# Joining the four chunks of an SSD scan into one stage schedule, and moving a state decay from VectorE to ScalarE

## The chip, the cores and the metric

The kernel runs on all 8 cores of one Trainium2 chip. Each core works on its own prompt sequence (2048 tokens) and its own 16 sample tokens, with the same weights. The metric is the device time of the slowest core in microseconds (us).

## What is computed

One layer of a hybrid decoder. Three mixers (a short gated convolution A, a Mamba-2 SSD branch B, a cross-attention C) read the same normalised input, are gated and merged, and a SwiGLU block follows. The change touches branch B alone. For the prompt it is a scan over chunks of 128 tokens:

```python
lmat = jnp.exp(jnp.where(causal, seg, -jnp.inf))
cb = jnp.einsum('bcign,bcjgn->bcijg', cr, br)
y_diag = jnp.einsum('bcijg,bcijgh,bcjghp->bcighp', cb, lmat, xdt)
def carry_step(s, inp):
    st, dec = inp
    return s * dec[..., None, None] + st, s
y_off = jnp.einsum('bcign,bcghpn,bcigh->bcighp', cr, s_prev, jnp.exp(acum))
```

For each sample token it is one step of the same recurrence, on a state of 32 heads x 64 x 128:

```python
s = s * jnp.exp(dtt * a)[..., None, None] + (dtt[..., None] * xt)[..., None] * bh[:, :, None, :]
return s, jnp.einsum('bhpn,bhn->bhp', s, ch)
```

## The kernel before

**Order.** The prompt is worked in four tiles of 512 tokens (`tile`): branch A, branch C, branch B, merge, SwiGLU, each fed by weight slabs that `wload` (L338) loads into a ring of 16 pages from POOL's queue. After the four tiles `sample` works on the 16 sample tokens. Instructions are added one by one through helpers (L344 `mm`, L347 `tr`, L355 `act`, L358 `tt`, L362 `ts`), so most rows of the trace bear a helper's line and are told apart by their tiles. Each engine runs its own instructions strictly in the order in which they were added. `Sched.add` sets a semaphore wait for each conflict of keys. For two instructions on one engine other than PE the wait is left out when they lie more than 6 places apart; two neighbours that write the same key do wait for each other. Whoever reads a PSUM bank also takes a lock on it (`psx`), so two readers of one bank follow each other.

**The scan in a tile** (in `branchB`). NS = 4 chunks `j`, and in each 4 groups `g4` of 8 heads. At the head of a chunk PE forms the four B.C products in bank 7 and ScalarE copies them to `CBs`. Then 14 steps `u` follow, and in each the stages are added in the order S5, S4, S3, S2, S1, A. In words:

- A(t), t = 0 to 7 (two per group): PE multiplies C by the carried state `Sbf` into bank `bo` (for even t), then one masked and three further products into bank 4 or 5; ScalarE takes the exponential into `Lt`; VectorE multiplies it by `CBs` into `MT`. The third buffer of `Lt` and `MT` is a piece of the tile `xdd`, so one in three shows under that name.
- S1(t), two steps later: PE multiplies `MT` by the inputs into bank `by`.
- S2(g): VectorE scales `bo` into `sA` (this frees `bo`), adds `by`, adds the skip term `sB` and multiplies by the gate into `yb`. POOL makes `sB`, the state input `xddg` and the decayed state `Sf`.
- S3(g): ScalarE squares `yb` into `sB` with a sum, then VectorE and ScalarE form the inverse root (`stat`). In this text "Square(k)" is the start of this squaring (`sB<-yb` on ScalarE) for the k-th group of the tile, k = 0 to 15.
- S4(g): ScalarE normalises into `ynb`; PE forms the state update in bank 7 and transposes `ynb` into bank 6.
- S5(g): VectorE adds the update to `Sf`, ScalarE copies it to `Sbf`, and VectorE and ScalarE move the four transposed blocks by turns to `G2`/`G3` (names `G<-ps,nw`).

S2 of group g is added in step 2g+4, S3 in 2g+5, S4 in 2g+6, S5 in 2g+7, so that the last steps of a chunk (u = 10 to 13) have neither S1 nor A. The next chunk's head comes behind them. After the fourth chunk come the output product with `w_ssm_out` and its gates.

**The sample state loop** (L1149 to L1171). For each of the 16 tokens: SyncE loads the next token's state (1 MB) into one of two buffers; PE broadcasts B and C into PSUM; VectorE multiplies the state by its decay into `t1_` (one instruction, `HB<-HB,G`); VectorE multiplies B by dt.x into `t2` (`MG<-ps,G`); POOL adds `t2` to `t1_` (`HB<-HB,MG`) and issues the store of the new state; VectorE multiplies by C into the same `t2` (`MG<-HB,ps`) and reduces it to `Ys` (L1171). There are two `t1_` buffers and one `t2`.

Of the kernel before, what the change touches and what calls it, by code (L numbers as in the profile page):

```python
# [8 lines left out]
AF = mybir.ActivationFunctionType  # L9
ALU = mybir.AluOpType  # L10
# [156 lines left out]
def build(with_sample=True, dbg=None, ntiles=NT, branches='ACB', stop=0):  # L167
# [95 lines left out]
    BT = sb("BT", [128, 4, T], BF16)  # L263
# [237 lines left out]
    def tile(ti, last):  # L501
# [126 lines left out]
        def branchB():  # L628
# [82 lines left out]
            BY = [0, 1]  # L711
            BO = [2, 3]
            BL = [4, 5]
            for j in range(NS):
                zk = [("zs", j, c) for c in range(4)]
                bc_ = 7
                for g4 in range(4):
                    mm(PS[bc_][:, g4 * 128:(g4 + 1) * 128], BT[:, g4, j * 128:(j + 1) * 128], CT[:, g4, j * 128:(j + 1) * 128], True, True,
                       [("BT", g4), ("CT", g4)], ("ps", bc_))
                cp("act", CBs[:].rearrange("p g i -> p (g i)"), PS[bc_][:, :], [("ps", bc_)], ["CBs"])  # L720

                def stageA(t, j=j):
                    g4, half = t // 2, t % 2
                    by, bo = BY[g4 % 2], BO[g4 % 2]
                    if half == 0:
                        mm(PS[bo][:, :], CT[:, g4, j * 128:(j + 1) * 128], Sbf[:, g4 * 512:(g4 + 1) * 512], True, True,
                           [("CT", g4), ("Sbf", g4)], ("ps", bo))
                    li = t % 3
                    bl = BL[t % 2]
                    h0 = g4 * 8 + half * 4  # L730
                    mm(PS[bl][:, :], ident_b, fap(mneg_b, [[0, 4], [1, 128]]), True, False, ["cstb"], ("ps", bl))
                    mm(PS[bl][:, :], ident_b, fap(nbh4[:, j, h0:h0 + 1], [[1, 4], [0, 128]]), False, False, ["cstb", ("nbh", j)], ("ps", bl))
                    mm(PS[bl][:, :], ident_b, fap(nbl4[:, j, h0:h0 + 1], [[1, 4], [0, 128]]), False, False, ["cstb", ("nbh", j)], ("ps", bl))
                    for hh in range(4):
                        h = h0 + hh
                        mm(PS[bl][:, hh * 128:(hh + 1) * 128], fap(dtab[:, j, h:h + 1], [[0, 128]]), tri_b, False, hh == 3,
                           [("dtab", j), "cstb"], ("ps", bl))
                    act(Lt[li][:].rearrange("p a b -> p (a b)"), PS[bl][:, :], AF.Exp, [("ps", bl)], [("Lt", li)])
                    tt("dve", MT[li][:], Lt[li][:], fap(CBs[:, g4, 0:1], [[0, 4], [1, 128]]), ALU.mult, [("Lt", li), "CBs"], [("MT", li)])

                def S1(t, j=j):
                    g4, half = t // 2, t % 2
                    by = BY[g4 % 2]
                    li = t % 3
                    for hh in range(4):
                        h = g4 * 8 + half * 4 + hh
                        hl = half * 4 + hh
                        mm(PS[by][:, hl * 64:(hl + 1) * 64], MT[li][:, hh, :], xs_v[:, j, h * 64:(h + 1) * 64], True, True,
                           [("MT", li)] + xsk, ("ps", by))

                def S2(g4, j=j, zk=zk):
                    by, bo = BY[g4 % 2], BO[g4 % 2]
                    i = g4 % 2
                    tt("dve", sA[i][:, :].rearrange("p (h q) -> p h q", h=8), PS[bo][:, :].rearrange("p (h q) -> p h q", h=8),
                       fap(eac4[:, j, g4 * 8:g4 * 8 + 1], [[1, 8], [0, 64]]), ALU.mult, [("ps", bo), ("eac4", j)], [("sA", i)])
                    tt("dve", sA[i][:, :], sA[i][:, :], PS[by][:, :], ALU.add, [("sA", i), ("ps", by)], [("sA", i)])
                    tt("pool", sB[i][:, :].rearrange("p (h q) -> p h q", h=8), xs_v[:, j, g4 * 512:(g4 + 1) * 512].rearrange("p (h q) -> p h q", h=8),
                       fap(hp[:, 2, g4 * 8:g4 * 8 + 1], [[1, 8], [0, 64]]), ALU.mult, xsk + ["hp"], [("sB", i)])
                    tt("dve", sA[i][:, :], sA[i][:, :], sB[i][:, :], ALU.add, [("sA", i), ("sB", i)], [("sA", i)])
                    tt("dve", yb[i][:, :], sA[i][:, :], zs_v[:, j, g4 * 512:(g4 + 1) * 512], ALU.mult, [("sA", i)] + zk, [("yb", i)])  # L760
                    xg = xddg[i]
                    tt("pool", xg[:].rearrange("p (h q) -> p h q", h=8), xs_v[:, j, g4 * 512:(g4 + 1) * 512].rearrange("p (h q) -> p h q", h=8),
                       fap(dsd4[:, j, g4 * 8:g4 * 8 + 1], [[1, 8], [0, 64]]), ALU.mult, xsk + [("dsd4", j)], [("xddg", i)])
                    tt("pool", Sf[:, g4 * 512:(g4 + 1) * 512].rearrange("p (h q) -> p h q", h=8),
                       Sf[:, g4 * 512:(g4 + 1) * 512].rearrange("p (h q) -> p h q", h=8),
                       fap(eac4[:, j, 32 + g4 * 8:32 + g4 * 8 + 1], [[1, 8], [0, 64]]), ALU.mult, [("Sf", g4), ("eac4", j)], [("Sf", g4)])

                def S3(g4):
                    i = g4 % 2
                    act(sB[i][:, :], yb[i][:, :], AF.Square, [("yb", i)], [("sB", i), ("gss", i)], accum=stat[:, 8 + i:9 + i])  # L770
                    rstd_from_ssq(8 + i, 12 + i, 512, 128, ("gss", i))

                def S4(g4, j=j):
                    i = g4 % 2
                    act(ynb[i][:, :], yb[i][:, :], AF.Copy, [("yb", i), ("gss", i)], [("ynb", i)], scale=stat[:, 12 + i:13 + i])
                    mm(PS[7][:, :], Btok[:, j, g4, :], xddg[i][:], True, True, ["Btok", ("xddg", i)], ("ps", 7))
                    pT = PS[6][:].bitcast(BF16)
                    for q in range(4):
                        tr(pT[:, q * 128:(q + 1) * 128], ynb[i][:, q * 128:(q + 1) * 128], ident_b, [("ynb", i), "cstb"], ("ps", 6))

                def S5(g4, j=j):
                    pT = PS[6][:].bitcast(BF16)
                    tt("dve", Sf[:, g4 * 512:(g4 + 1) * 512], Sf[:, g4 * 512:(g4 + 1) * 512], PS[7][:, :], ALU.add,
                       [("Sf", g4), ("ps", 7)], [("Sf", g4)])
                    cp("act", Sbf[:, g4 * 512:(g4 + 1) * 512], Sf[:, g4 * 512:(g4 + 1) * 512], [("Sf", g4)], [("Sbf", g4)])
                    for q in range(4):
                        ch = g4 * 4 + q
                        dstb = G2 if ch < 8 else G3
                        dk = ("G2" if ch < 8 else "G3", ch % 8)
                        if q % 2 == 0:  # L790
                            ts("dve", dstb[:, ch % 8, j * 128:(j + 1) * 128], pT[:, q * 128:(q + 1) * 128], nw[:, ch:ch + 1], None,
                               ALU.mult, None, [("ps", 6), "nw"], [dk])
                        else:
                            act(dstb[:, ch % 8, j * 128:(j + 1) * 128], pT[:, q * 128:(q + 1) * 128], AF.Copy, [("ps", 6), "nw"], [dk],
                                scale=nw[:, ch:ch + 1])

                for u in range(14):
                    for g4 in range(4):
                        if u == 2 * g4 + 7:
                            S5(g4)  # L800
                    for g4 in range(4):
                        if u == 2 * g4 + 6:
                            S4(g4)
                    for g4 in range(4):
                        if u == 2 * g4 + 5:
                            S3(g4)
                    for g4 in range(4):
                        if u == 2 * g4 + 4:
                            S2(g4)
                    if 2 <= u < 10:  # L810
                        S1(u - 2)
                    if u < 8:
                        stageA(u)
            if last:
                for q in range(16):
                    b = nb()
# [85 lines left out]
    def sample():  # L902
# [249 lines left out]
        for bi in range(P):  # L1152
            if bi + 1 < P:
# [5 lines left out]
            mm(PS[bB][:, :], oh, bctok[:, 0:512], True, True, ["cstf", "bctok"], ("ps", bB))  # L1159
            bC = nb()  # L1160
            mm(PS[bC][:, :], oh, bctok[:, 512:1024], True, True, ["cstf", "bctok"], ("ps", bC))
            tt("dve", t1_.rearrange("p (a n) -> p a n", a=16), St_.rearrange("p (a n) -> p a n", a=16),
               fap(decT[:, 0, bi:bi + 1], [[16, 16], [0, 128]]), ALU.mult, [sk_, "decsT"], [tk_])
            tt("dve", fap(t2[:, 0:1], [[512, 4], [128, 4], [1, 128]]), fap(PS[bB][:, 0:1], [[128, 4], [0, 4], [1, 128]]),
               fap(dtT[:, 0, bi:bi + 1], [[64, 4], [16, 4], [0, 128]]), ALU.mult, [("ps", bB), "dtsT"], ["t2"])
            tt("pool", t1_, t1_, t2, ALU.add, [tk_, "t2"], [tk_])
# [129 lines left out]
```

How the kernel before makes its waits and increments, by code:

```python
        def run(e, eng):  # L120
            water = {}
            for op in self.by_eng[e]:
                need = {}
                for o in op.deps:
                    k = o.sem.num
                    if water.get(k, 0) >= o.val:
                        continue
                    if k not in need or need[k][1] < o.val:
                        need[k] = (o.sem, o.val)
                for k, (s, v) in need.items():
                    eng.wait_ge(s, v)
                    water[k] = v
                ins = op.fn(eng)
                if op.is_dma:
                    ins.then_inc(op.sem, 16)
                elif op.signal:
                    ins.then_inc(op.sem, 1)
            if e == "sp":
                for s, cnt in self.slot_count.items():
                    eng.wait_ge(ssem[s], 16 * cnt)
```

## Time and profile before

| | us |
|---|---|
| median of 2 runs | 3812.38 (3811.84 to 3812.92) |
| profiled execution | 3815.4 |
| its span on the slowest core (7) | 3813.9 |
| spans of the other cores | 3745.8 to 3808.3 |
| PE busy in it | 2273.0 (60%) |
| VectorE, ScalarE, POOL busy | 1231.7, 959.6, 770.2 |

The profiled execution lies 3 us above the median, and 1.5 us of it lie outside the span. Times in the rows are microseconds from the start of the span of core 7. In a row of the timeline the columns are: start, length, engine, line, operation, output and inputs, shapes, count, and in brackets how long the engine had sat idle and who released it.

### The profile page before, as it was taken

What the parts mean: (1) busy time and instruction counts of PE and PEld (TensorE: products, weight loads), DVE (VectorE), ACT (ScalarE), POOL (GpSimd) and SP (SyncE); (2) the same over time, 40 slices, a digit from 0 to 9 for tenths busy, and PEclk for the clock granted to TensorE, in tenths of its full rate; (3) what the DMA queues carried; (4) which work ended last, traced back from release to release, by engine and by line L of the source; (5) the groups of instructions that cost most, each with busy time, mean ns of one, the idle gap of its engine ahead of it and who ended that gap; (6) DMA issues with size and microseconds to landing.
All of it is one profiled execution on the core that took longest, in us unless ns stands there. A gap on an engine that the chain in (4) does not pass through costs nothing.

```text
span 3813.9 us, 39632 instructions; the slowest of 8 cores (3745.8 to 3813.9 us)
## 1 busy us (share of the span) xinstructions
PE 2273.0 (60%) x11878; PEld 1046.6 (27%) x11878; DVE 1231.7 (32%) x2656; ACT 959.6 (25%) x2088; POOL 770.2 (20%) x759
## 2 busy tenths in 40 slices
PE   4778457758784578679646777793488322232112
PEld 2333223223332233234322333342233210120011
DVE  2224542122245321322452213335421114346610
ACT  2134431111344210223441112343311103310000
POOL 1211221312103222211132302103213010013310
PEclk8889668879886689789767888896688655555555
DMA  8974037979630489997007999750289696575498
GB/s 148 110 88 64 1 40 90 116 119 124 87 46 1 50 95 125 127 112 111 2 1 90 90 125 139 95 77 1 35 107 122 109 157 204 166 136 154 138 156 132
DMA packets 615311, 370.48 MB, mean 97 GB/s; under 512 B 394768, under 2 KB 586768, under 8 KB 615088
## 3 DMA queue, kind: packets, MB, share of 16 engines
q0 software_dynamic: 584752, 286.10, 61.1%
q1 hardware_dynamic: 30352, 81.85, 6.6%
q8 instruction: 101, 1.65, 0.2%
q14 instruction: 106, 0.87, 0.1%
HBM read 608.44 MB, written 29.14 MB: 167 GB/s over the span
## 4 chain that ended last, share of the span: by engine, by line
DMA 35%; PE 30%; DVE 12%; issue 11%; ACT 7%; POOL 3%; DVEq 1%; SPq 0%; ACTq 0%; POOLq 0%
PE ps L344 29%; DMA WRb<-w_in 13%; DMA WRb<-w_ffn_gate 6%; DMA WRb<-w_ffn_down 5%; DMA WRb<-w_ffn_up 4%; DVE MG L358 3%; DVE sA L358 2%; DMA WRb<-w_sc_out 2%; DMA WRb<-w_ssm_out 2%; POOL HB L358 2%; PE ps L347 1%; POOL WRb L338 1%; ACT sB L355 1%; DVE acs L1080 1%; DMA ostg<-st_sconv 1%
## 5 line engine op out<-in xcount | busy, mean ns | idle before, releaser
L344 PE MATMUL ps<-G,WRb 128*128 128x512 bf16 (+2 forms) x6432 | 1251.0, 350 | 363.6 <-DMA WRb<-w_in 151.8
L344 PEld LDWEIGHTS ps<-G,WRb 128*128 128x128 bf16 x6432 | 542.4, 102 | 1028.1 <-issue 531.9
L338 POOL DMA_DIRECT2D WRb<-w_in x269 | 235.9, 886 | 1458.9 <-PE ps L344 839.5
L355 ACT ACTIVATE sA<-ps 128x512 f32<-128x512 f32 (+1 forms) x294 | 142.7, 486 | 868.3 <-PE ps L344 848.7
L344 PE MATMUL ps<-WRb,HB 128*128 128x512 bf16 x960 | 232.1, 408 | 54.0 <-DMA WRb<-w_ffn_down 36.0
L355 ACT ACT_TABLE_LOAD x56 | 71.8, 1283 | 404.5 <-DVE eac L364 229.1
L358 POOL TENSOR_TENSOR sB<-HB,hp 128x512 f32<-128x512 bf16 x64 | 66.7, 1041 | 518.4 <-ACT sB L355 411.8
L358 DVE TENSOR_TENSOR HB<-sA,ps 128x512 bf16<-128x512 f32 x88 | 60.5, 688 | 342.5 <-PE ps L344 336.8
L347 PE MATMUL ps<-cstb,ynb 128*128 128x128 bf16 x256 | 34.9, 284 | 216.0 <-ACT ynb L355 159.5
L355 ACT ACTIVATE junk<-X 128x1024 bf16<-128x1024 f32 (+1 forms) x53 | 56.0, 1056 | 383.8 <-DVE X L358 306.7
L344 PEld LDWEIGHTS ps<-WRb,HB 128*128 128x128 bf16 x960 | 98.5, 104 | 187.6 <-issue 90.9
L358 DVE TENSOR_TENSOR sB<-sA,ps 128x512 f32<-128x512 f32 (+1 forms) x80 | 46.7, 584 | 302.9 <-ACT sA L355 275.6
L344 PE MATMUL ps<-WRb,G 128*128 128x512 bf16 (+3 forms) x728 | 138.0, 350 | 9.6 <-DMA WRb<-w_merge_o 8.6
L347 PE MATMUL ps<-cstb,xnb 128*128 128x128 bf16 (+1 forms) x152 | 17.9, 292 | 208.7 <-DVE xnb L373 208.7
L358 DVE TENSOR_TENSOR X<-X,ps 128x512 f32<-128x512 f32 (+1 forms) x68 | 46.7, 687 | 287.9 <-PE ps L344 287.9
L358 DVE TENSOR_TENSOR MG<-HB,ps 128x1024 f32<-128x1024 f32 (+1 forms) x48 | 75.7, 1577 | 170.2 <-POOL HB L358 78.4
L338 POOL DMA_DIRECT2D WRb<-w_ffn_up x94 | 85.6, 911 | 210.3 <-DMA WRb<-w_ffn_gate 183.8
L344 PE MATMUL ps<-X,cstf 16*128 16x512 f32 x64 | 62.3, 1103 | 107.0 <-DVE MG L358 107.0
L344 PE MATMUL ps<-xb,dg 128*128 128x512 bf16 x384 | 102.7, 391 | 26.2 <-DVE xb L370 18.5
L338 POOL DMA_DIRECT2D WRb<-w_ffn_gate x94 | 85.7, 912 | 132.2 <-PE ps L344 72.2
L362 DVE TENSOR_SCALAR dg<-cstb,cw 128x128 bf16<-128x128 bf16 x384 | 100.0, 260 | 32.4 <-DVE dg L362 2.0
L358 POOL TENSOR_TENSOR HB<-HB,MG 128x2048 f32<-128x2048 f32 x16 | 71.7, 4483 | 170.8 <-DVE MG L358 170.8
(183 smaller groups left out, 2980.4 us busy)
## 6 DMA issues: line engine op xcount, KB each, us to landing
WRb<-w_in POOLq DMA_DIRECT2D x72, 1024.0 KB, 13.0
WRb<-w_in POOLq DMA_DIRECT2D x192, 256.0 KB, 9.1
WRb<-w_ffn_down POOLq DMA_DIRECT2D x20, 1408.0 KB, 12.7
WRb<-w_ffn_gate POOLq DMA_DIRECT2D x88, 256.0 KB, 15.6
WRb<-w_ffn_up POOLq DMA_DIRECT2D x88, 256.0 KB, 15.7
WRb<-w_ssm_out POOLq DMA_DIRECT2D x20, 1024.0 KB, 11.1
HB<-cache_k SPq DMA_DIRECT2D x16, 1024.0 KB, 6.2
HB<-cache_v SPq DMA_DIRECT2D x16, 1024.0 KB, 8.6
```

The source lines that it names most:

```text
L338: S.add("pool", lambda g: g.dma_start(out=dst, in_=src), writes=[("wl", ser)] + [("wl", q) for q in prev], slot=("w", start))
L344: S.add("pe", lambda g: g.matmul(out, lhsT, rhs, start=start, stop=stop), reads=reads, writes=[pskey])
L347: S.add("pe", lambda g: g.transpose(out, in_, idn), reads=reads, writes=[pskey])
L355: S.add("act", lambda g: g.activation(out=out, in_=in_, func=func, scale=scale, **kw), reads=reads, writes=writes)
L358: S.add(eng, lambda g: g.tensor_tensor(out=out, in0=in0, in1=in1, op=op), reads=reads, writes=writes)
L362: S.add(eng, lambda g: g.tensor_scalar(out=out, in0=in0, scalar1=s1, scalar2=None, op0=op0), reads=reads, writes=writes)
L1080: S.add("dve", lambda g: g.tensor_reduce(out=ssc, in_=prod.rearrange("p (a d) -> p a d", d=256), op=ALU.add, axis=AX), reads=["prod"], wri ...
```

## The change

The first part keeps each stage of the scan, but collects them for all four chunks and runs one step counter U over the tile, U = 0 to 39: A of chunk j in steps 8j to 8j+7, S1 two steps behind it, S2 to S5 of group g of chunk j in steps 8j + 2g + 4 to 8j + 2g + 7. The chunk's head (`pro`) is added in step 8j between S1 and A; it now uses bank 4, which is also that of A(0), in place of bank 7, which S4 and S5 use. The index of the `Lt`/`MT` buffers runs on through the tile.

The second part replaces VectorE's one multiplication of the 128x2048 state by 16 ScalarE activations of 128x128, each with its own per-partition scale.

```diff
--- before.py
+++ after.py
@@ -711,13 +711,16 @@
             BY = [0, 1]
             BO = [2, 3]
             BL = [4, 5]
+            CH = []
             for j in range(NS):
                 zk = [("zs", j, c) for c in range(4)]
-                bc_ = 7
-                for g4 in range(4):
-                    mm(PS[bc_][:, g4 * 128:(g4 + 1) * 128], BT[:, g4, j * 128:(j + 1) * 128], CT[:, g4, j * 128:(j + 1) * 128], True, True,
-                       [("BT", g4), ("CT", g4)], ("ps", bc_))
-                cp("act", CBs[:].rearrange("p g i -> p (g i)"), PS[bc_][:, :], [("ps", bc_)], ["CBs"])
+
+                def pro(j=j):
+                    bc_ = BL[0]
+                    for g4 in range(4):
+                        mm(PS[bc_][:, g4 * 128:(g4 + 1) * 128], BT[:, g4, j * 128:(j + 1) * 128], CT[:, g4, j * 128:(j + 1) * 128], True, True,
+                           [("BT", g4), ("CT", g4)], ("ps", bc_))
+                    cp("act", CBs[:].rearrange("p g i -> p (g i)"), PS[bc_][:, :], [("ps", bc_)], ["CBs"])
 
                 def stageA(t, j=j):
                     g4, half = t // 2, t % 2
@@ -725,7 +728,7 @@
                     if half == 0:
                         mm(PS[bo][:, :], CT[:, g4, j * 128:(j + 1) * 128], Sbf[:, g4 * 512:(g4 + 1) * 512], True, True,
                            [("CT", g4), ("Sbf", g4)], ("ps", bo))
-                    li = t % 3
+                    li = (8 * j + t) % 3
                     bl = BL[t % 2]
                     h0 = g4 * 8 + half * 4
                     mm(PS[bl][:, :], ident_b, fap(mneg_b, [[0, 4], [1, 128]]), True, False, ["cstb"], ("ps", bl))
@@ -741,7 +744,7 @@
                 def S1(t, j=j):
                     g4, half = t // 2, t % 2
                     by = BY[g4 % 2]
-                    li = t % 3
+                    li = (8 * j + t) % 3
                     for hh in range(4):
                         h = g4 * 8 + half * 4 + hh
                         hl = half * 4 + hh
@@ -794,23 +797,20 @@
                             act(dstb[:, ch % 8, j * 128:(j + 1) * 128], pT[:, q * 128:(q + 1) * 128], AF.Copy, [("ps", 6), "nw"], [dk],
                                 scale=nw[:, ch:ch + 1])
 
-                for u in range(14):
-                    for g4 in range(4):
-                        if u == 2 * g4 + 7:
-                            S5(g4)
-                    for g4 in range(4):
-                        if u == 2 * g4 + 6:
-                            S4(g4)
-                    for g4 in range(4):
-                        if u == 2 * g4 + 5:
-                            S3(g4)
-                    for g4 in range(4):
-                        if u == 2 * g4 + 4:
-                            S2(g4)
-                    if 2 <= u < 10:
-                        S1(u - 2)
-                    if u < 8:
-                        stageA(u)
+                CH.append((pro, stageA, S1, S2, S3, S4, S5))
+            for U in range(8 * NS + 8):
+                for st_i, off in ((6, 7), (5, 6), (4, 5), (3, 4)):
+                    for j in range(NS):
+                        for g4 in range(4):
+                            if U == 8 * j + 2 * g4 + off:
+                                CH[j][st_i](g4)
+                gt = U - 2
+                if 0 <= gt < 8 * NS:
+                    CH[gt // 8][2](gt % 8)
+                if U < 8 * NS:
+                    if U % 8 == 0:
+                        CH[U // 8][0]()
+                    CH[U // 8][1](U % 8)
             if last:
                 for q in range(16):
                     b = nb()
@@ -1159,8 +1159,9 @@
             mm(PS[bB][:, :], oh, bctok[:, 0:512], True, True, ["cstf", "bctok"], ("ps", bB))
             bC = nb()
             mm(PS[bC][:, :], oh, bctok[:, 512:1024], True, True, ["cstf", "bctok"], ("ps", bC))
-            tt("dve", t1_.rearrange("p (a n) -> p a n", a=16), St_.rearrange("p (a n) -> p a n", a=16),
-               fap(decT[:, 0, bi:bi + 1], [[16, 16], [0, 128]]), ALU.mult, [sk_, "decsT"], [tk_])
+            for a16 in range(16):
+                act(t1_[:, a16 * 128:(a16 + 1) * 128], St_[:, a16 * 128:(a16 + 1) * 128], AF.Copy, [sk_, "decsT"], [tk_],
+                    scale=decT[:, a16, bi:bi + 1])
             tt("dve", fap(t2[:, 0:1], [[512, 4], [128, 4], [1, 128]]), fap(PS[bB][:, 0:1], [[128, 4], [0, 4], [1, 128]]),
                fap(dtT[:, 0, bi:bi + 1], [[64, 4], [16, 4], [0, 128]]), ALU.mult, [("ps", bB), "dtsT"], ["t2"])
             tt("pool", t1_, t1_, t2, ALU.add, [tk_, "t2"], [tk_])
```

## Rows read from the trace of the kernel before

**Rows 1.** The page: busy us, share of the span and instructions by engine.

```profile
PE 2273.0 (60%) x11878; PEld 1046.6 (27%) x11878; DVE 1231.7 (32%) x2656; ACT 959.6 (25%) x2088; POOL 770.2 (20%) x759
```

**Rows 2.** The page: the chain that ended last, by engine.

```profile
DMA 35%; PE 30%; DVE 12%; issue 11%; ACT 7%; POOL 3%; DVEq 1%; SPq 0%; ACTq 0%; POOLq 0%
```

**Rows 3.** Windows, first chunk's span: busy us (instructions) by engine, PEclk, DMA share, GB/s.

```profile
382.10:424.30 42.20, 19.27 (x124) 10.77 (x125) 21.56 (x45) 17.52 (x44) 12.98 (x12) 0.66 0.00 1
```

**Rows 4.** Timeline, ScalarE: the Squares of chunk 1, the next, and chunk 4's.

```profile
393.83 0.63 ACT L355 ACTIVATE sB<-yb 128x512 f32<-128x512 f32 x1 [0.48 <-DVE yb L358]
...
403.61 0.62 ACT L355 ACTIVATE sB<-yb 128x512 f32<-128x512 f32 x1
...
412.23 0.62 ACT L355 ACTIVATE sB<-yb 128x512 f32<-128x512 f32 x1
...
419.44 0.62 ACT L355 ACTIVATE sB<-yb 128x512 f32<-128x512 f32 x1
...
434.27 0.63 ACT L355 ACTIVATE sB<-yb 128x512 f32<-128x512 f32 x1 [0.47 <-DVE yb L358]
...
515.12 0.63 ACT L355 ACTIVATE sB<-yb 128x512 f32<-128x512 f32 x1 [0.33 <-issue]
...
524.19 0.62 ACT L355 ACTIVATE sB<-yb 128x512 f32<-128x512 f32 x1
...
532.82 0.62 ACT L355 ACTIVATE sB<-yb 128x512 f32<-128x512 f32 x1
...
539.23 0.62 ACT L355 ACTIVATE sB<-yb 128x512 f32<-128x512 f32 x1
```

**Rows 5.** Timeline, all engines: what lies between the first two Squares of chunk 1.

```profile
396.91 0.59 PE L347 MATMUL ps<-cstb,ynb 128*128 128x128 bf16 x4 [3.16 <-ACT ynb L355]
...
397.77 0.59 PE L344 MATMUL ps<-Sbf,CT 128*128 128x512 bf16 x1
...
400.16 0.60 ACT L355 ACTIVATE Lt<-ps 128x512 bf16<-128x512 f32 x1 [3.39 <-PE ps L344]
...
401.20 0.68 DVE L358 TENSOR_TENSOR Sf<-Sf,ps 128x512 f32<-128x512 f32 x1
```

**Rows 6.** Timeline, PE to ScalarE: the same stage A at the higher clock.

```profile
391.31 0.38 PE L344 MATMUL ps<-Sbf,CT 128*128 128x512 bf16 x1 [1.72 <-DVE sA L358]
...
392.76 0.60 ACT L355 ACTIVATE Lt<-ps 128x512 bf16<-128x512 f32 x1 [2.87 <-PE ps L344]
```

**Rows 7.** Timeline, a chunk's head: the B.C products, their copy, the next product.

```profile
382.14 0.58 PE L344 MATMUL ps<-CT,BT 128*128 128x128 bf16 x4 [1.52 <-DVE acs L370]
...
382.82 0.60 ACT L355 ACTIVATE CBs<-ps 128x512 bf16<-128x512 f32 x1 [0.20 <-PE ps L344]
```

**Rows 8.** Timeline, one token of the sample state loop.

```profile
3426.84 4.48 POOL L358 TENSOR_TENSOR HB<-HB,MG 128x2048 f32<-128x2048 f32 x1 [7.29 <-DVE MG L358]
...
3431.91 1.18 POOL L1167 DMA_DIRECT2D sssm<-HB  x1 [0.59 <-POOL HB L358]
...
3436.15 2.28 DVE L358 TENSOR_TENSOR HB<-HB,G 128x2048 f32<-128x2048 f32 x1
3438.35 2.28 DVE L358 TENSOR_TENSOR MG<-ps,G 128x2048 f32<-128x2048 f32 x1
```

**Rows 9.** The tile HB in that loop: ns min/median/max, first and last start.

```profile
L358 DVE TENSOR_TENSOR HB<-HB,G x16: 2279/2281/2291, 3408.2 to 3617.6; 128x2048 f32<-128x2048 f32 x16
L358 POOL TENSOR_TENSOR HB<-HB,MG x16: 4482/4483/4487, 3412.9 to 3622.5; 128x2048 f32<-128x2048 f32 x16
```

**Rows 10.** Groups of ScalarE by shape: busy us, mean ns.

```profile
L355 ACT ACTIVATE G<-ps,nw 128x128 bf16<-128x128 bf16 x128 | 46.2, 361 | 44.4 <-DVE G L362 34.0 <-PE ps L344 9.6 <-PE ps L347 0.8
```

**Rows 11.** Timeline, ScalarE: two neighbours that take turns on one bank.

```profile
3165.15 0.37 ACT L355 ACTIVATE ostg<-ps 1x256 f32<-1x256 f32 x1 [0.99 <-PE ps L344]
3165.62 0.16 ACT L355 ACTIVATE stat<-ps 1x1 f32<-1x1 f32 x1
```

**Rows 12.** The tile HB again: from issue to landing, loads and stores.

```profile
DMA to landing us min/median/max: 6.0/6.1/10.4
```

## Prediction

> **What bounds the kernel now.** First the page. No engine is near full, PE is busy 60% [rows 1], and the chain that ended last is DMA 35%, PE 30%, VectorE 12% [rows 2]: long stages wait for weights, others for products. Shares alone say nothing of the two places that the change touches, so these are read from the timeline.
>
> The first place is the scan of branch B, four times (once a tile). The window over its first chunk, 42.2 us, has PE busy 19.3, VectorE 21.6, ScalarE 17.5 and POOL 13.0 us, and no DMA [rows 3]. Nobody is the bound by work; a chain that hops between engines is. I measure it by the distance between Squares [rows 4]: 9.78, 8.62, 7.21, and then 14.83 us over the chunk's border. The 14.83 is what the change goes for: the pipe drains and fills again. The other twelve borders and inner gaps repeat this; the sixteen gaps from a chunk's first Square to its second run from 8.97 to 9.78 (first and last in tile 1: 9.78 and 9.07), eleven within 0.03 of 9.77, one 9.70, four at the end of a tile 8.97 to 9.32, mean 9.59. In a tile Square(0) to Square(15) takes 539.23 - 393.83 = 145.4; over the four tiles the mean is 145.0.
>
> The second place is the sample state loop. A token is one closed chain: POOL's add, VectorE's product with C, the reduction, the decay product, the B product, POOL's add again [rows 8]. Its period is (3622.5 - 3412.9) / 15 = 13.97 us [rows 9]. ScalarE does nothing there.
>
> **Part 1, the joined scan.** No work is removed. What decides is how long a gap between Squares is when the stages A are present all the time. The rows show one such gap in each chunk, the first one, since it holds the exponentials of A(5) and A(6); the second gap holds A(7) alone, the third none. I follow the gap of chunk 1 from its Square at 393.83 [rows 4]. The sum, root and odd exponential on ScalarE, then `MT` and `sA` on VectorE free the bank `bo`, and PE's product with the state starts at 397.77, after 3.94. The further products let the even exponential start at 400.16, after 2.39; behind it `MT`, and `Sf` starts at 401.20, after 1.04 [rows 5]. The copy to `Sbf` and the four moves to `G2`/`G3` by turns lead to the next Square at 403.61, after 2.41 [rows 4]. The sum is 9.78. In the new order every middle gap has this chain.
>
> The one variable link is PE's. From the state product to the exponential it is 400.16 - 397.77 = 2.39 us, where most of it runs at 1.2 GHz (the first row shows 0.59 a product), and 392.76 - 391.31 = 1.45 us at 2.4 GHz (0.38 a product) [rows 5, 6]. With the short link VectorE's own four products of S2 come to bound, and the gap is the 8.97 seen at the ends of tiles. So a full gap costs 9.77 at the low clock and 8.97 at the high one. The granted clock over a chunk is 0.66 [rows 3], a mixture. Before each burst of PE the trace has about 3 us of idleness (3.16 here) [rows 5], and the new order leaves a like pause, so I take the mean of the sixteen, 9.6, nearer the low end.
>
> Which gaps are full? Groups k to k+1 use the exponentials 2k+5 and 2k+6 of 32, so k = 0 to 12 are full: 13 gaps. The last two keep the values of today's tile end, 532.82 - 524.19 = 8.63 and 539.23 - 532.82 = 6.41 [rows 4], together 15.0.
>
> The head of chunks 2 to 4 now stands inside full gaps. From the start of its products to its copy is 382.82 - 382.14 = 0.68, the copy takes 0.60 [rows 7]. A(0)'s further products use the same bank 4 and must wait for the copy, so 1.28 plus about 0.05 for the wait; 0.43 of it lies beside the state product, which uses another bank. That is 0.9 a head, 2.7 a tile, bounded below by 0.6 each (the copy alone) and above by 1.3. Queued behind that wait on PE are the products of A(0) and A(1) and nothing else; their exponentials are what the chain waits for, so I count it whole. For the first head of a tile the same bank costs 0.3 more, as the copy ends at 383.42 and the next product began just before 383: 1 us for four tiles.
>
> New tile: 13 x 9.6 + 15.0 + 2.7 = 142.5, against 145.0: 2.5 a tile, 10 in all, less 1 is **9 us**. With 9.77 it is 144.7, gain 0.3 a tile, 1 in all, and with the first heads nothing. With 8.97 and 0.6 a head it is 133.4, gain 46, less 1 is 45.
>
> Other waits are hidden. A of chunk j+1 now reads `Sbf` one step after S5 wrote it. But PE's transposes of S4 stand ahead of that product and wait for `ynb`, which ScalarE makes after that copy. POOL's three instructions a group (3.2 us, released by the Square two groups ahead) fit into a gap of 9. Without cover they would be late only beyond 9. After the scan POOL's weight loads stand behind its last scan instruction, which Square(13) releases, and the last two gaps don't change, so the output product keeps its distance and the gain passes to the end.
>
> **Part 2, the decay on ScalarE.** VectorE loses 16 instructions of 2.28 us [rows 9]; in the chain one counts by its start to start, 3438.35 - 3436.15 = 2.20 [rows 8]. It stood in the chain since VectorE is in order and was kept from running ahead. Fifteen periods: 15 x 2.20 = 33.0, so a period is 11.8.
>
> ScalarE gets 16 x 16 activations. No row has exactly this form; the nearest is 128x128 bf16 with a per-partition scale, 0.361 us [rows 10]. All 16 write one key and are neighbours, so each waits for the one before it: such a pair shows 3165.62 - 3165.15 = 0.47 for a length of 0.37, so 0.10 more [rows 11]. So 0.46 each, 7.4 a token. Bounds: 0.37 (no extra) and 0.73, twice the row, are 5.9 and 11.7. Cover: POOL, VectorE and PE go on meanwhile. The Trainium skill, "ScalarE: Activation LUTs", section "Rules for kernel authors", advises VectorE for a product and gives about 0.3 us an activation plus 0.83 ns an element. By that, an estimate from the page, it would be 16 x 0.41 = 6.5 us against VectorE's one instruction; the sum here would be the same, as either is covered. The row, at 0.36 against 0.41, is near the page.
>
> Is it covered? `t1_` of token b can be written only when the store of token b-2 has landed. Counted from the start of add b-2: the add ends at 4.5, the store is issued at 5.1 (3431.91 - 3426.84) [rows 8], lands 6.1 later [rows 12] at 11.2, ScalarE ends at 18.6, and add b starts two periods on, at 23.5. Slack 4.9, so nothing is lost even with a landing of 10.4. SyncE's load of the state waits for ScalarE's reading, earlier in the period than needed. What is late next is the chain itself, POOL and VectorE by turns.
>
> The first token is bare: today the decay product starts at 3408.2 when the state lands, and the add at 3412.9 [rows 9]. Now the add starts at 3408.2 + 7.4 = 3415.6, a loss of 2.8. Net 33.0 - 2.8 = **30 us**, bounds 26 (at 0.73 an activation, where ScalarE is just not the bound and the start costs 7.0) and 32.
>
> **Sum.** 9 + 30 = 39 us, off the profiled execution 3815.4 - 39 = 3776, off its span of 3813.9 it is 3775; off the median of 3812.4 it is **3773**.
>
> **Rivals.**
> - A, the pipelining buys nothing: PE comes into every gap after a pause and at 1.2 GHz, the gap is 9.77 and the heads eat the rest. For it: eleven of sixteen such gaps. Against: the four at tile ends. 3812.4 - 30 = 3782.
> - B, denser work keeps PE at 2.4 GHz: gain 45 in the scan, 3812.4 - 75 = 3737. For it: 8.97 is seen; against: the pauses remain.
> - C, the decay is only part hidden: activations of 0.8 us make ScalarE the bound at 12.8 us a token; 15 x (13.97 - 12.8) = 17, less 8 at the start, with the scan's 9: 3794. Only twice the row's length gives this.
> - D, the other side: ScalarE becomes the bound of the loop at its 16 activations. It decides from 14.0 us a token, 0.87 an activation: there the loop gains nothing and the start costs 9, what the scan brings. Price at 1.0 us an activation: 16.0 a token, 15 x 2.0 = 31 lost plus 11 at the start, less 9: 3845. Against: 0.361 in the row.
>
> **Chances.** Forecast 0.45, A 0.33, B 0.10, C 0.07, D 0.05. The range must hold 8 in 10: 3745 to 3792 holds the forecast, A, and a part of B, and takes in the bounds of both sums between the extremes of the clock. Two per cent, 76 us, is about what a measurement of this kernel tells from no change. Faster by more needs B whole (below 3736): 0.04. Slower by more (above 3888) is a worse D: 0.02. Within: 0.94.
>
> **What would show it.** In the changed trace: no gap of 14 us between Squares inside a tile; thirteen gaps of 9.0 to 9.8, with about 0.9 more in three of them; Square(0) to (15) 134 to 145 us; a granted clock near 0.66 if A, clearly above if B; 256 activations of 128x128 at 0.3 to 0.4 us; POOL's adds 11.8 us apart. Wrong would be the forecast if a full gap were longer than 9.8, if a new wait for `Sbf`, bank 4 or `CBs` stood in the waits with more than 1 us a chunk, or if VectorE waited for ScalarE in the sample loop.

## The result and the profile after

The changed kernel takes 0.9947 of the time before (95% interval 0.9929 to 0.9964): 0.5% or about 20 us less (14 to 27), where 39 were forecast. In some executions of either kernel one or both dies showed a lower granted clock and took longer; ratios and medians here leave these out. The changed kernel's median is then 3799 us, above the forecast of 3773 and above its range of 3745 to 3792. A second comparison on another occasion gave 0.9938 (0.9917 to 0.9959), 24 us. More executions of the kernel before put its median at 3816 to 3819 us and not at the 3812 of the first two, so 4 to 7 us of the distance between forecast and measurement are the base; the rest is the gain, which was about half of what I said. The profiled execution has a span of 3810.4 us on its slowest core (3).

The Squares of the first tile, ScalarE's timeline of the kernel after (start, length, engine, line, operation, names, shapes, idle before):

```profile
387.42 0.63 ACT L355 ACTIVATE sB<-yb 128x512 f32<-128x512 f32 x1 [0.42 <-DVE yb L358]
...
397.20 0.62 ACT L355 ACTIVATE sB<-yb 128x512 f32<-128x512 f32 x1
...
407.60 0.62 ACT L355 ACTIVATE sB<-yb 128x512 f32<-128x512 f32 x1
...
417.36 0.62 ACT L355 ACTIVATE sB<-yb 128x512 f32<-128x512 f32 x1
...
427.11 0.62 ACT L355 ACTIVATE sB<-yb 128x512 f32<-128x512 f32 x1
```

These answer [rows 4]. The gaps are now 9.78, 10.40, 9.76, 9.75. The 14.83 us at the border is gone, but so are the short gaps of 8.62 and 7.21: four gaps were 40.4 us and are 39.7. One gap from inside, all engines:

```profile
417.36 0.62 ACT L355 ACTIVATE sB<-yb 128x512 f32<-128x512 f32 x1
...
420.30 0.58 PE L347 MATMUL ps<-cstb,ynb 128*128 128x128 bf16 x4 [4.04 <-ACT ynb L355]
...
421.27 0.58 PE L344 MATMUL ps<-Sbf,CT 128*128 128x512 bf16 x1 [0.18 <-DVE sA L358]
...
423.66 0.60 ACT L355 ACTIVATE Lt<-ps 128x512 bf16<-128x512 f32 x1 [3.65 <-PE ps L344]
...
424.70 0.68 DVE L358 TENSOR_TENSOR Sf<-Sf,ps 128x512 f32<-128x512 f32 x1
```

From Square to state product 3.91, to the exponential 2.39, to `Sf` 1.04, to the next Square 2.41: link by link the gap of [rows 5]. PE idles 4.04 us ahead of the transposes, and its products run at 0.58, the length of 1.2 GHz; from the state product to the exponential (421.27 to 423.66) the granted clock is 0.50. The windows over a whole first tile of scan, kernel before and kernel after (window, its length, busy us and count of PE, PE's loads, VectorE, ScalarE, POOL, then granted clock, DMA share, GB/s):

```profile
393.80:539.20 145.40, 60.63 (x394) 33.06 (x394) 76.98 (x148) 61.05 (x150) 47.42 (x44) 0.66 0.08 10
```

```profile
387.40:531.50 144.10, 69.61 (x395) 36.69 (x394) 77.38 (x148) 59.67 (x151) 47.14 (x44) 0.66 0.08 10
```

The same work in 1.3 us less at the same granted clock. PE is busy 9 us longer in it for the same number of products, so these are longer on the mean: more of them fall into the time at the low clock.

The sample state loop, POOL's timeline after, first and last of 16 adds and the second store:

```profile
3436.10 4.49 POOL L358 TENSOR_TENSOR HB<-HB,MG 128x2048 f32<-128x2048 f32 x1 [58.78 <-ACT HB L355]
...
3453.15 1.18 POOL L1168 DMA_DIRECT2D sssm<-HB  x1 [0.59 <-POOL HB L358]
...
3615.76 4.48 POOL L358 TENSOR_TENSOR HB<-HB,MG 128x2048 f32<-128x2048 f32 x1 [5.67 <-DVE MG L358]
```

The period is (3615.76 - 3436.10) / 15 = 11.98 us, against 13.97 [rows 9]. The decay's group of ScalarE on the page:

```profile
L355 ACT ACTIVATE HB<-HB,G 128x128 f32<-128x128 f32 x256 | 102.7, 401 | 81.5 <-DMA sssm<-HB 49.3
```

256 activations of 0.401 us, and 49.3 us of idleness in which ScalarE waited for a store to land, as the plan had it (`t1_` is free when the store two tokens back has landed).

For the whole program I cut every core of every profiled execution at the same marks: the Squares 0 and 15 of each tile, the first and the last activation of the attention loop of the sample, the first and the last add. Means over the eight cores, in us:

| stretch | before | after | joined scan only | decay only | decay only, again | after, again |
|---|---|---|---|---|---|---|
| four scans, Square(0) to (15) | 579.7 | 576.6 | 576.4 | 580.2 | 580.0 | 576.4 |
| end of attention loop to first add | 109.3 | 113.4 | 110.5 | 112.8 | 112.6 | 113.0 |
| first add to last | 209.6 | 179.7 | 209.7 | 180.0 | 180.0 | 179.7 |
| all the rest | 2882 | 2900 | 2900 | 2876 | 2879 | 2874 |

The loop is the same to 0.4 us from core to core and between executions; a scan after is 143.8 to 144.4, and before 143.7 to 146.2; the second row scatters by several us from core to core. The rest scatters by 27 us between executions: these are mostly the stretches that wait for weights. One small piece of the rest does change with the kernel. From the last `acs<-ps` copy ahead of a tile's scan to Square(0), summed over the four tiles, it is 48.0 to 48.2 us in the three columns with separate chunks and 50.0 to 50.4 in the three with joined ones. The joined scan so gives back 2 us ahead of its first Square.

### The profile page after: what moved, and what is told of

It reads as the page before. It is cut to its first block, busy times and chain, and to the rows that moved or that the text cites. A ratio compares the mean times of both kernels' runs of the same rounds, so it can differ in the third digit from the quotient of the medians.

```text
span 3810.4 us, 39993 instructions; the slowest of 8 cores (3728.9 to 3810.4 us)
## 1 busy us (share of the span) xinstructions
PE 2329.4 (61%) x11878; PEld 1067.0 (28%) x11878; DVE 1199.2 (31%) x2640; ACT 1057.0 (28%) x2344; POOL 769.3 (20%) x759
## 4 chain that ended last, share of the span: by engine, by line
DMA 35%; PE 31%; DVE 12%; issue 9%; ACT 8%; POOL 3%; DVEq 1%; ACTq 0%; SPq 0%; POOLq 0%
PE ps L344 30%; DMA WRb<-w_in 16%; DMA WRb<-w_ffn_gate 7%; DMA WRb<-w_ffn_down 4%; DVE MG L358 3%; DMA WRb<-w_ffn_up 3%; POOL HB L358 2%; POOL WRb L338 1%; DMA WRb<-w_ssm_out 1%; PE ps L347 1%; ACT sB L355 1%; ACT Lt L355 1%; DMA WRb<-w_merge_o 1%; DVE Sf L358 1%; DVE acs L1080 1%
## 5 line engine op out<-in xcount | busy, mean ns | idle before, releaser
L344 PE MATMUL ps<-WRb,HB 128*128 128x512 bf16 x960 | 240.2, 418 | 46.4 <-DMA WRb<-w_ffn_down 25.8
L347 PE MATMUL ps<-cstb,xnb 128*128 128x128 bf16 (+1 forms) x152 | 17.9, 292 | 209.7 <-DVE xnb L373 209.7
L355 ACT ACTIVATE HB<-HB,G 128x128 f32<-128x128 f32 x256 | 102.7, 401 | 81.5 <-DMA sssm<-HB 49.3
L355 ACT ACTIVATE G<-ps 128x512 bf16<-128x512 f32 (+5 forms) x103 | 54.5, 529 | 203.0 <-PE ps L344 90.6
```

The source lines that it names most:

```text
L344: S.add("pe", lambda g: g.matmul(out, lhsT, rhs, start=start, stop=stop), reads=reads, writes=[pskey])
L347: S.add("pe", lambda g: g.transpose(out, in_, idn), reads=reads, writes=[pskey])
L355: S.add("act", lambda g: g.activation(out=out, in_=in_, func=func, scale=scale, **kw), reads=reads, writes=writes)
```

## The experiments

**One part alone.** In `e1_scan` the changed kernel with VectorE's decay put back:

```diff
-            for a16 in range(16):
-                act(t1_[:, a16 * 128:(a16 + 1) * 128], ..., scale=decT[:, a16, bi:bi + 1])
+            tt("dve", t1_..., St_..., fap(decT[:, 0, bi:bi + 1], [[16, 16], [0, 128]]), ALU.mult, [sk_, "decsT"], [tk_])
```

> Only the joined scan; the decay of the sample state stays on VectorE. Theory (the gap between Squares is a closed chain through all engines of 9.77 us, and joining the chunks only makes all gaps that long): in a tile Square(0) to Square(15) takes 144.1 instead of 145.0 us, thirteen gaps of 9.77, three of them 0.5 to 0.7 longer for the chunk's head, the last two 8.62 and 6.41; gain 4 us in all, ratio 0.999. Rival (the joined scan gave more than its own stretch, through earlier weight loads, and the other part gave less): ratio 0.995 or lower. Rival (it costs time elsewhere): ratio above 1.001.

Measured 0.9994 (0.9971 to 1.0018), so 2 us gained, give or take 9. Its stretch is 144.1, 143.9, 144.4 and 144.0 us, 3.3 us less than before in the four. The joined scan is worth 3 us in that stretch and, with the 2 us ahead of Square(0), about 1 us in all.

`e2_act` is the other half, the kernel before with only the ScalarE decay:

> Only the decay on ScalarE; the scan is that of before. Theory: the period of a token falls from 13.97 to 11.98 us, the first add starts 8.3 instead of 4.7 us after the state is there, 26 us gained in the stretch, ratio 0.993. Rival (all that was measured of the whole change, 0.9947, is this part, and the scan gives nothing or loses): 0.995 with no gain in the first experiment. In neither case should the stretch itself differ from that of the whole change, 188.0 us from the first state landing to the last add.

Measured 0.989 (0.9858 to 0.9922), 42 us. The stretch gave 26, as expected (0.1 to 0.3 us apart from the whole change). The comparison gave more than its stretch, and the whole change less than its stretches (29): one of the two had to be scatter, or the joined scan cost something elsewhere. So both were run again side by side, `e5_whole` without any edit and `e6_act_again` as `e2_act`.

> The changed kernel itself, beside the decay-only kernel on one chip. The touched stretches of its trace give 29 us over before (3 in the four scans, 26 in the sample state), ratio 0.9924; the comparison on record gave 0.9947. Theory (the rest is scatter of the weight-bound stretches, which differ by 10 to 20 us between executions of one kernel): ratio between 0.991 and 0.995, and within 0.003 of the decay-only kernel. Rival (the joined scan costs some 15 us in stretches that it does not touch): the decay-only kernel is faster by more than 0.003.

> The decay-only kernel once more. Its touched stretch gives 26 us, ratio 0.993; the first comparison gave 0.989. Scatter: this one comes out near 0.993 and the whole change beside it within 0.003. Rival: again 0.989, with the whole change at 0.995.

Measured 0.9938 (0.9917 to 0.9959) for the whole and 0.9947 (0.9927 to 0.9967) for the decay alone. They are within 0.001 of each other, the 0.989 did not come back, and a loss of some 15 us elsewhere through the joined scan is not seen. With the 2 us ahead of Square(0) the stretches of the whole change make 27 and not 29. The comparisons gave 20 (14 to 27) and 24 (16 to 32). A few more microseconds given back in the weight-bound stretches can't be excluded.

**Is it PE's clock?** `e3_warm` gives PE more to do while it waits for `ynb`:

```diff
                     mm(PS[7][:, :], Btok[:, j, g4, :], xddg[i][:], ...)
+                    for _f in range(12):
+                        mm(PS[6][:, 256:512], ident_b, fap(mneg_b, [[0, 2], [1, 128]]), True, True, ["cstb"], ("ps", 6))
```

> The changed kernel with 12 further products of 128x256 on PE ahead of each S4's transposes, in the unused half of bank 6; their results are read by nobody. PE does more work, in the pause in which it waits for ynb. Theory of the clock (each burst starts at 1.2 GHz after a pause, and that is 0.8 us of each of 13 gaps a tile): the products' lengths fall from 0.59-0.63 to 0.38, the gap goes from 9.77 toward 8.97, Square(0) to (15) from 144 to about 134 us, 40 us in all. Rival (the chain is bound by the other engines' hand-overs whatever the clock): gap unchanged within 0.1. Rival (the filler itself stands in PE's way): gap above 9.8.

Measured 0.9834 (0.9792 to 0.9875). The Squares of its first tile, and the window over that scan:

```profile
386.96 0.63 ACT L355 ACTIVATE sB<-yb 128x512 f32<-128x512 f32 x1 [0.47 <-DVE yb L358]
395.93 0.62 ACT L355 ACTIVATE sB<-yb 128x512 f32<-128x512 f32 x1
405.44 0.62 ACT L355 ACTIVATE sB<-yb 128x512 f32<-128x512 f32 x1
415.21 0.62 ACT L355 ACTIVATE sB<-yb 128x512 f32<-128x512 f32 x1
```

```profile
387.00:522.40 135.40, 81.06 (x573) 48.59 (x571) 76.69 (x148) 59.58 (x150) 47.21 (x44) 0.84 0.08 10
```

The granted clock is 0.84 in place of 0.66 and the plain gap 8.97; about one gap in five keeps the long link from state product to exponential and stays near 9.77 (one of the three here). The four scans are 541 us, 35 less than after; with the 29 of the whole change that is 64 us, and the ratio says 63. So the clock is 0.8 us of each full gap, and it is PE's idle time that costs it, as the filler does nothing but fill it. Useless work made the kernel faster.

**Is it the order of the stages?** `e4_order` is the changed kernel with another order of emission in a step:

```diff
-                S5, S4, S3, S2        (the loop over st_i, off)
+                st_(6, 7)             # S5
+                st_(3, 4)             # S2
                 ... S1, then the head and A as before ...
+                st_(4, 5)             # S3
+                st_(5, 6)             # S4
```

> The changed kernel with another order of the stages within a step: S5, S2, S1, head and A, S3, S4 in place of S5, S4, S3, S2, S1, head and A. Same work. Theory (the gap is set by the order in which the in-order engines meet the stages: sum of squares, root, ynb, transposes, products of A, exponential, Sf, moves, one after the other): A's products no longer stand behind the transposes, nor the odd exponential behind the root, so a gap falls from 9.77 to about 8.5 us at the low clock; 13 gaps in four tiles, about 60 us. Rival (the order within a step does not matter, since the recurrence over the state or the engines' work sets the gap): within 0.2 of 9.77.

Measured 0.9733 (0.9686 to 0.978), 102 us less than before. Its Squares, core 2:

```profile
387.80 0.62 ACT L355 ACTIVATE sB<-yb 128x512 f32<-128x512 f32 x1
396.13 0.63 ACT L355 ACTIVATE sB<-yb 128x512 f32<-128x512 f32 x1
404.22 0.63 ACT L355 ACTIVATE sB<-yb 128x512 f32<-128x512 f32 x1
412.31 0.63 ACT L355 ACTIVATE sB<-yb 128x512 f32<-128x512 f32 x1
421.02 0.63 ACT L355 ACTIVATE sB<-yb 128x512 f32<-128x512 f32 x1
```

Full gaps of 8.1 to 8.9 us with the same work and a clock of 0.65 over that tile. The four scans are 500 us, 76 less than after. PE's products of A no longer queue behind transposes that wait for ScalarE: the state product starts 1.72 after its Square and not 3.9 (rows below, under "All together"). The odd exponential no longer stands behind the root; what each of the two brings was not measured apart.

`e8_order_nojoin` asks what the join is worth under that order: the kernel before, its chunks apart and its decay on VectorE, with only the stages within `for u in range(14)` put in the new order.

> The kernel before, chunks not joined and the decay on VectorE, with only the order of stages in a step changed as in the reordering experiment. Theory (the order in a step sets the gap, the join only fills the border): gaps 8.4, 7.2, 6.4 and about 14 at the border, Square(0) to (15) about 130 us against 145 before and 125 with both; about 60 us gained, ratio 0.984. Rival (the new order pays only when the stages of two chunks overlap): above 140 us.

Measured 0.9923 (0.9896 to 0.995, on two executions), 29 us, where I had said 0.984. Its Squares:

```profile
391.03 0.62 ACT L355 ACTIVATE sB<-yb 128x512 f32<-128x512 f32 x1
399.22 0.63 ACT L355 ACTIVATE sB<-yb 128x512 f32<-128x512 f32 x1
406.45 0.62 ACT L355 ACTIVATE sB<-yb 128x512 f32<-128x512 f32 x1
413.67 0.62 ACT L355 ACTIVATE sB<-yb 128x512 f32<-128x512 f32 x1
428.63 0.62 ACT L355 ACTIVATE sB<-yb 128x512 f32<-128x512 f32 x1
```

Gaps 8.19, 7.23, 7.22, and 14.96 at the border: Square(0) to (15) is 136.1 us on the mean of tiles and cores, not 130; the inner gaps did not shrink to 6.4, nor the border to 14. The order alone brings 35 us in four tiles. On top of it the join brings (136.1 - 125.1) x 4 = 44 us, where under the old order it brought 3 (of either, 1 to 2 us are given back ahead of Square(0)). The two edits need each other: a join pays by the difference between a chunk's total of short gaps plus border (37.6 here) and four full gaps (about 34 with a head), and under the old order these were 40.4 and 39.7.

**The sample loop.** `e7_t2` adds a second `t2` (the free half of `MG`) and puts the next token's B product ahead of this token's C product:

```diff
+        T2 = [(t2, "t2"), (prod, "prod")]
             tt("pool", t1_, t1_, t2_, ALU.add, ...)        # token bi, then its store
+            front(bi + 1)     # PE broadcasts, decay, B product into the other t2
             tt("dve", t2_, t1_, C product ...)              # token bi, then the reduction
```

> The changed kernel with a second t2 buffer in the sample state loop, and the next token's B product added ahead of the C product of the present one. Same work. Theory (after the change a token is still one chain of POOL's add and three VectorE instructions, 11.98 us, in which VectorE idles during the add): the B product moves beside the add and the period falls by its 2.4 us to about 9.6, bound then by the landing of the store two tokens back plus ScalarE's 8 us, (11.2 + 8.0) / 2; 15 x 2.4 = 36 us less than the whole change. Rival (ScalarE's activations at 0.5 us are already the bound): the period stays 11.98. Rival (POOL and VectorE slow each other when they overlap): the add grows above 4.5 us and the period falls by less than 1.

Measured 0.9843 (0.9805 to 0.988). The loop takes 150.4 us on the mean, 10.0 a token and not 9.6, 29 us less than after. Three adds in a row:

```profile
3475.50 4.50 POOL L358 TENSOR_TENSOR HB<-HB,MG 128x2048 f32<-128x2048 f32 x1 [1.54 <-ACT HB L355]
3480.93 1.17 POOL L1178 DMA_DIRECT2D sssm<-HB  x1 [0.92 <-POOL HB L358]
3487.81 4.49 POOL L358 TENSOR_TENSOR HB<-HB,MG 128x2048 f32<-128x2048 f32 x1 [5.71 <-ACT HB L355]
3492.94 1.17 POOL L1178 DMA_DIRECT2D sssm<-HB  x1 [0.63 <-POOL HB L358]
3495.60 4.50 POOL L358 TENSOR_TENSOR HB<-HB,MG 128x2048 f32<-128x2048 f32 x1 [1.49 <-ACT HB L355]
```

POOL now waits for ScalarE each time (16 activations from 3459.49 on, 0.49 apart, end at 3467.3; the add starts at 3467.51), and two periods are 20.1 us: the landing and the activations (11.2 + 8.0 = 19.2 expected) have become the bound. The add is not slowed by the overlap (4.49 to 4.50).

`e11_keys` takes away what makes the 16 activations wait for each other: 15 of them write keys of their own, which POOL's add reads.

```diff
-                    [tk_], scale=decT[:, a16, bi:bi + 1])
+                    [tk_ if a16 == 0 else (tk_, a16)], scale=decT[:, a16, bi:bi + 1])
```

> The changed kernel, only the 16 activations of the decay freed from waiting for each other. Theory (their start to start of 0.5 us is the length of 0.40 plus 0.1 for the wait): 0.30 to 0.40 from start to start, first add 1.6 to 3 us earlier after the state's landing than 8.3, period of a token unchanged at 11.98 since they are covered. Rival (0.5 is what ScalarE needs for such an activation): first add unchanged.

```profile
3407.99 9.46 ACT L355 ACTIVATE HB<-HB,G 128x128 f32<-128x128 f32 x32
...
3412.98 4.50 POOL L358 TENSOR_TENSOR HB<-HB,MG 128x2048 f32<-128x2048 f32 x1 [55.62 <-ACT HB L355]
```

32 activations in 9.46 us are 0.30 each from start to start, and the first add follows the first activation by 5.0 us in place of 8.3. The loop stays at 179.7 us: while the decay is covered, its price is paid by the first token only. Whole times were not compared for this kernel.

**All together.** `e9_best` has the new order, the second `t2` and the separate keys; `e10_best_warm` adds 8 filler products to it.

> The changed kernel with the new order of stages, the second t2 buffer, and 16 keys for the 16 activations of the decay, so that they no longer wait for each other. Theory (the stretches are closed chains and add up): scans as in the reordering experiment, 125 us each (80 less than before in all), the loop 150 us or less (60 less), first add some 1 us later; together about 138 us less than before, ratio 0.964. Rival (weight loads take back what the scan gives): ratio above 0.97 with the stretches as short as that.

> The same with 8 further products of 128x256 ahead of each S4's transposes, whose results nobody reads. Theory (what is left of the spread of the gaps, 8.1 to 8.9, is PE's clock): gaps of 8.1 throughout, Square(0) to (15) about 120 us, 20 less than without in all. Rival (PE's idle time ahead of the transposes is down to 1 us, so the filler stands in the chain): gaps above 8.9.

`e9_best` measured 0.9619 (0.9584 to 0.9653), 146 us less than before. Scans 123.9, 125.6, 124.4, 125.8 us, loop 145.5: together 144 us less than before in those stretches (80 and 64), so what they gained arrived. In the loop the activations are 3 us shorter a token than in `e7_t2`, but the loop gained only 5 us: the stores landed later, 6.5 to 7.9 us after their issue (medians of the eight cores) against 6.5 to 6.8. `e10_best_warm` measured 0.9623 (0.957 to 0.9677), no difference; its scans sum to 497 us against 500. Two windows over a first scan, without the filler and with it:

```profile
390.90:514.50 123.60, 62.53 (x395) 33.32 (x395) 80.78 (x147) 58.99 (x151) 49.81 (x44) 0.66 0.09 11
```

```profile
393.70:518.00 124.30, 73.69 (x515) 44.58 (x513) 81.77 (x147) 58.93 (x151) 49.87 (x44) 0.80 0.09 11
```

The clock rose from 0.66 to 0.80, but this scan did not shorten and the four lost only 3 us; I had expected 120 us a tile, 20 less in all. That is not because PE were off the chain. Two neighbouring gaps of `e4_order`, core 2, with Squares at 404.22, 412.31 and 421.02, state product and even exponential:

```profile
405.94 0.38 PE L344 MATMUL ps<-Sbf,CT 128*128 128x512 bf16 x1 [3.59 <-DVE sA L358]
...
407.35 0.60 ACT L355 ACTIVATE Lt<-ps 128x512 bf16<-128x512 f32 x1 [1.56 <-PE ps L344]
...
414.03 0.59 PE L344 MATMUL ps<-Sbf,CT 128*128 128x512 bf16 x1 [2.61 <-DVE sA L358]
...
416.42 0.60 ACT L355 ACTIVATE Lt<-ps 128x512 bf16<-128x512 f32 x1 [2.54 <-PE ps L344]
```

In the gap of 8.09 the link is 1.41 long, at a granted clock of 0.87; in the gap of 8.71 it is 2.39, at 0.50. So the clock at this link still makes a gap 8.7 instead of 8.1, 0.6 us where it was 0.8 under the old order. Over all cores, 195 of the 368 full gaps of `e9_best` whose products the trace holds have a link above 2.25 us, and their median is 8.72; with the filler 120 of 368 have it. Part of what this should bring is lost again: gaps of 8.9 behind a short link become more (40 in place of 13). What holds these was not settled.

## Why the prediction was right or wrong

**The reading of the scan was right and its middle value wrong.** That a closed chain of hand-overs bounds the scan, that a full gap is the first gap of a chunk, 9.77 at the low clock and 8.97 at the high one, that thirteen gaps are full and the last two 8.6 and 6.4: the traces have each of them (8.97 in `e3_warm`, the others in the trace after). Then "I take the mean of the sixteen, 9.6". Four of these sixteen stood at the end of a tile, and those four alone were short. The new gaps are all like the other twelve: 9.75 to 9.78 in the first tile, where no head is inside. The mean mixed two situations. Before, timeline of PE and ScalarE in the short gap from 515.12 of [rows 4]:

```profile
517.93 0.38 PE L347 MATMUL ps<-cstb,ynb 128*128 128x128 bf16 x4 [1.59 <-ACT ynb L355]
...
519.06 0.38 PE L344 MATMUL ps<-Sbf,CT 128*128 128x512 bf16 x1 [0.62 <-DVE sA L358]
...
520.74 0.60 ACT L355 ACTIVATE Lt<-ps 128x512 bf16<-128x512 f32 x1 [2.95 <-PE ps L344]
```

PE had paused 1.59 us ahead of the transposes and not 3.16 [rows 5], and the link took 1.68 and not 2.39. On the eight cores of that execution, 33 of 128 such gaps were short, all with a pause of 1.2 to 1.9 us and a link below 1.8; the others had a pause of 2.8 us or more, all but one, and a link of 2.3 or more. The text had the reason at hand: it said that the pause of PE stays, and in the middle of the joined scan it is even longer (4.04 us). The step that failed is the choice of 9.6 for the full gap in spite of that; 9.77 was right. This was rival A, at 0.33, with a scan gain near nothing; measured are 3 us inside the stretch and 1 with the first heads, where the sum had 9. The third experiment shows that the clock was the right variable, and that rival B's 8.97 needs PE's pause filled.

**The head of a chunk** was costed at 0.9 and is 0.7: the gap with a head is 10.2 to 10.6, on the mean 10.47. The wait stands where it was put, at bank 4, PE for ScalarE's copy. Timeline after, the head in the gap from 397.20:

```profile
401.12 0.63 PE L344 MATMUL ps<-Sbf,CT 128*128 128x512 bf16 x1
...
401.48 0.60 ACT L355 ACTIVATE CBs<-ps 128x512 bf16<-128x512 f32 x1 [1.63 <-PE ps L344]
...
402.22 0.59 PE L344 MATMUL ps<-cstb 128*128 128x512 bf16 x1 [0.47 <-ACT CBs L355]
```

The masked product starts 5.02 after its Square, against 4.29 in the gap without a head. The head's copy started at 401.48, 0.36 after the state product, so more of it lay beside that product than I had counted. The first heads of the tiles, costed at 1 us in all, took 2.

**The sample loop** was costed at 30 and gave 26. The period fell by 1.99 and not by 2.20: 15 x 0.21 = 3. Before, reduction, decay product and B product followed each other without a wait, 2.20 from start to start each ([rows 8] for the last two); now the B product comes straight behind the reduction and overwrites the `t2` that this reads, so it must wait for its end. Removing a link put two conflicting neighbours side by side. Rows after: reduction to B product is 2.39 us. The first row names ScalarE as the releaser of the C product; the C product of the next token, with the same 4.96 of idleness, names POOL, whose add is what it needs (the one at 3448.07 ends at 3452.56). VectorE does not wait for ScalarE here.

```profile
3452.87 2.29 DVE L358 TENSOR_TENSOR MG<-HB,ps 128x2048 f32<-128x2048 f32 x1 [4.96 <-ACT HB L355]
...
3455.26 2.29 DVE L1172 TENSOR_REDUCE G<-MG 128x16 f32<-128x2048 f32 x1
...
3457.65 2.29 DVE L358 TENSOR_TENSOR MG<-ps,G 128x2048 f32<-128x2048 f32 x1
...
3464.90 2.29 DVE L358 TENSOR_TENSOR MG<-HB,ps 128x2048 f32<-128x2048 f32 x1 [4.96 <-POOL HB L358]
```

The activations cost 0.49 from start to start and not 0.46 (0.401 long, not 0.361, plus the 0.1 for the wait), 7.9 a token, so the first add came 8.3 us after the first activation (3427.8 to 3436.1) in place of 4.7, 3.6 later and not 2.8 (2.7 by the prediction's own numbers). They were covered, as said, and rivals C and D fell.

**The sum.** The scan brought 1 for 9 (3 inside the stretch, less 2 ahead of it) and the loop 26 for 30, which makes 27 for 39. The largest part of the miss is the full gap taken at 9.6: 52 gaps x 0.17 are 9 us. The comparisons show 20 and 24, with intervals that reach 27 and 32. The remaining distance is not explained: the weight-bound stretches scatter by more than it. The base was off too: the forecast of 3773 us started from two executions at 3812, where later medians of the kernel before were 3816 to 3819. A forecast in absolute time on two executions should have had a range wider by this.

That the change is within 2% was right. That it does not touch the stretches outside was right but for the 2 us of the first heads, as far as can be seen.

## What to carry to other kernels

When stages of in-order engines are joined over a border, cost the full step, not the border: if a step in the middle of the pipe takes as long as the fill and drain it replaces, spread over the steps, nothing is gained. Cost that step at the clock that PE will have there: a mean over situations with short and long pauses is the price of neither. Look first for the chain that closes a step (here transposes and an exponential queued behind a root on another engine) and cut it by the order of emission; the join then pays (44 us in the four scans instead of 3). And when a link is taken out of a chain, look at the two neighbours that it kept apart.

## What the runs showed of the hardware

- In the old order, 12 products of 128x256 in PE's pauses raised the granted clock of the scan from 0.66 to 0.84 and took 35 us off the kernel's four scans, in a kernel where PE is busy 61% of the time; in the new order 8 such products, 0.66 to 0.80, took off 3 us.
- The same products of one stage A took 1.3 to 1.8 us from state product to exponential where most of them ran at the high clock, and 2.3 to 2.4 us at the low one (full gaps of the trace before; `e4_order` has 1.41 and 2.39).
- An activation of 128x128 f32 from SBUF to SBUF with a per-partition scale was 0.40 us long and 0.49 from start to start when each waits for the one before, and 0.39 long and 0.29 from start to start when none does (`e11_keys`): the wait cost more than the 0.1 that lies between end and next start, as the engine otherwise overlaps two of them.
- POOL's add of 128x2048 took 4.48 to 4.50 us whether VectorE was idle or, in `e7_t2`, worked on a product from PSUM beside it; in the scan after, a VectorE product of 128x512 bf16 beside POOL's work took 0.96 (at 399.41) in place of 0.43 (at 424.36, POOL idle).
